# A feed-forward output product cut by token tiles instead of by output columns

## The chip, the cores and the metric

The kernel runs on one core of one Trainium2 chip, in fp32 throughout: matrix products are made of fp32r parts, as described below. The metric is the device time of one execution in microseconds. The kernel before has a median of 1441.0 us over 3 runs.

## What is computed

One step of an encoder layer on 640 tokens (512 of a prompt, 128 of eight samples of 16) with a model width of 1024. Two feed-forward blocks stand around a token mixer; each is followed by a gated, normalised residual. The parts that the change touches are the second half of the feed-forward block and what comes right behind it:

```python
def swiglu(h, w_in, w_out):
    gate, up = jnp.split(h @ w_in, 2, axis=-1)
    return (jax.nn.silu(gate) * up) @ w_out          # D_FF = 2816 -> 1024

def residual(x, out, g, gate, weight):
    return x + weight * gate[:, None, :] * rms_norm(out, g)

def trunk_layer(...):
    x = residual(x, swiglu(modulate(x, ...), w_ffn1_in, w_ffn1_out), ..., 0.5)
    heads, new_state = mixer(modulate(x, ...))       # modulate begins with rms_norm(x)
    x = residual(x, heads @ w_out, ..., 1.0)
    x = residual(x, swiglu(modulate(x, ...), w_ffn2_in, w_ffn2_out), ..., 0.5)
    return x, new_state
```

The root mean square of a token's output row is taken over all 1024 columns. So nothing of the residual of a token can be finished before all columns of its output are.

## The kernel before

The program is written engine by engine; each engine runs its instructions in the order of the code and waits on counting semaphores. Tokens are 5 tiles of 128 (`NT`), tiles 0 to 3 of the prompt, tile 4 of the samples. The hidden width is 22 blocks of 128 (`FT`), kept transposed in `act_t` (`ACTT`), one block of 640 tokens after the other. Numbers f = 0 and f = 1 are the two feed-forward blocks.

The output product (`ffn_out`) runs over the 22 hidden blocks in 11 turns (`OUT_TURNS`) of two slots, s = 0 and s = 1. For a slot, SP loads a block of the weight into `w_raw` (`RAW`); ACT rounds it to fp32r (`w_hi`) and the tokens' block too (`act_hi`), in `out_hi`; DVE subtracts to get the low parts (`w_lo`, `act_lo`), in `out_lo`; and PE makes three matmuls for each pair of a token tile and 512 columns: high times high, high tokens with low weight, low tokens with high weight. `k_landed`, `k_hi`, `k_lo` and `k_mm` count the loads, the high parts, the low parts and the slots that PE is done with. Each slot has one place in every buffer, so ACT may write the next turn's high parts of slot s only when PE is done with that slot (`k_mm[s]`), and SP may reload its `w_raw` only when both low parts are made.

The 640 x 1024 output takes 10 banks of PSUM, of which there are 8, 512 fp32 columns each. The kernel before therefore makes the product in two halves of columns: 11 turns with all 5 token tiles and columns 0 to 511 (banks 0 to 4), then 11 turns with the same tiles and columns 512 to 1023. Per slot that is 15 matmuls of 128x512. In the first 6 turns of f = 0 other small products (adaLN parameters, `ada_mm`, `ada_tr`) stand between the slots; a few transposes for the gate rows (`gate_mms`) stand in turns 6 and 7.

Behind each half ACT squares the five banks with a sum over the columns (`y_squares`), and DVE multiplies them with the gate rows into `y` (`y_gated`). Behind the second half follow, in this order: `inverse_mean` on DVE and a square root on ACT; on DVE `resid` += `y` times the root, five tiles of 128x1024; and, for f = 0, the next norm: ACT squares each new `resid` tile, DVE and ACT invert and take the root, DVE scales three tiles into `x_norm` and ACT two; only then PE transposes `x_norm` for the mixer (`norm` on PE waits for all five tiles). For f = 1 the new `resid` tiles are stored instead (L641), and that ends the kernel.

The product in front of this one (`ffn_in`) ends with sums on DVE that empty banks 0 to 6, a silu on ACT and the last block of `act_t` on DVE; `out_hi(0, 0)` and `out_lo(0, 0)` are placed among these last steps.

All three matmul forms are recorded under one line, the helper `mm` at L1079, and all subtractions under L1723.

## Time and profile before

| | us |
|---|---|
| median of 3 runs (1438.35 to 1442.01) | 1441.0 |
| the profiled execution | 1432.52 |
| its span, first to last instruction | 1430.7 |
| PE busy in the span | 1317.1 (92%) |
| DVE busy | 828.3 (58%) |
| ACT busy | 573.1 (40%) |
| mean granted TensorE clock | 0.952 |

The span is what the trace shows; the execution's own time is 1.8 us longer. The profiled execution is 8.5 us below the median of the runs, so a sum made from the trace is a difference to be applied to both, and not a time by itself. Busy shares are averages over the whole kernel. The stages of interest here are the two output products, at 359 to 522 us and 1265 to 1419 us of the span, and the stretches right behind them.

### The profile page before, as it was taken

Reading aid. Unit: us, or ns where it says so; the run is one execution under the profiler, and the core shown is the slowest. Engines: PE = TensorE matmul, PEld = TensorE weight load, DVE = VectorE, ACT = ScalarE, POOL = GpSimd, SP = SyncE. Lnnn points to the kernel's source line nnn. Section 1 sums busy time; section 2 is a strip of 40 time slices with the busy share of each in tenths; the row PEclk is TensorE's granted clock in tenths of the full one; section 3 lists DMA queues with packets and bytes.
Section 4 is the critical chain, followed back from the end, with each engine's and each line's share of the span. In section 5 each row is a group of like instructions: output and inputs, shape, how many; then the busy total and the mean of one; then the engine's idle time right before and its main releaser. Section 6 shows DMA issues by size and latency. Waiting matters only on the chain.

```text
span 1430.7 us, 23707 instructions
## 1 busy us (share of the span) xinstructions
PE 1317.1 (92%) x8072; PEld 1147.1 (80%) x8072; DVE 828.3 (58%) x1445; ACT 573.1 (40%) x1131; POOL 319.4 (22%) x276
## 2 busy tenths in 40 slices
PE   4999999999999969999997688969999999999996
PEld 2889999999778858888875355858899999988885
DVE  2666767776435455513335875338777777754545
ACT  4533434433334355322112465336444444433433
POOL 0443343433100000000100604004444444510000
PEclk9999999999999989999975698989999999999998
DMA  9545454544433322221220523112223322212232
GB/s 316 166 148 154 153 159 143 153 147 132 163 109 96 132 63 91 88 88 59 104 60 0 156 75 123 31 73 60 74 73 88 88 87 73 74 59 74 95 132 111
DMA packets 167003, 152.71 MB, mean 107 GB/s; under 512 B 10361, under 2 KB 139777, under 8 KB 166954
## 3 DMA queue, kind: packets, MB, share of 16 engines
q1 hardware_dynamic: 165610, 148.24, 33.0%
q0 software_dynamic: 1344, 3.81, 1.0%
q8 instruction: 31, 0.51, 0.2%
q14 instruction: 18, 0.15, 0.0%
HBM read 142.72 MB, written 9.05 MB: 106 GB/s over the span
## 4 chain that ended last, share of the span: by engine, by line
PE 79%; DVE 10%; issue 4%; ACT 4%; DMA 2%; DVEq 0%; POOL 0%; SPq 0%; ACTq 0%; POOLq 0%
PE ps L1079 76%; DVE resid L1942 1%; DVE w_sums_lo L1723 1%; DVE h_sums_lo L1723 1%; DVE max_den L2217 1%; DMA resid<-in_x_sample 1%; DMA w_raw<-in_w_ffn_in 1%; DVE act_t L1834 1%; DVE silu_gate L1827 1%; DVE w_lo L1723 1%; DVE probs L2226 1%; ACT x_norm L661 1%; PE ps L1121 0%; DVE y L1905 0%; ACT modulated_pairs L712 0%
## 5 line engine op out<-in xcount | busy, mean ns | idle before, releaser
L1079 PE MATMUL ps<-h_sums_hi,w_sums_hi 128*128 128x320 f32 x1216 | 378.0, 315 | 15.3 <-ACT silu_gate L731 5.0
L1079 PE MATMUL ps<-h_sums_hi,w_sums_lo 128*128 128x320 f32 x1216 | 370.7, 309 | 0.0
L1079 PE MATMUL ps<-h_sums_lo,w_sums_hi 128*128 128x320 f32 x1216 | 370.5, 309 | 0.0
L1079 PEld LDWEIGHTS ps<-h_sums_hi,w_sums_hi 128*128 128x128 f32 x1216 | 227.2, 188 | 31.9 <-issue 20.7
L1723 DVE TENSOR_TENSOR w_lo<-w_raw,w_hi 128x512 fp32r<-128x512 f32 (+3 forms) x106 | 99.0, 934 | 230.7 <-ACT w_hi L805 156.1
L1079 PEld LDWEIGHTS ps<-h_sums_lo,w_sums_hi 128*128 128x128 f32 x1216 | 227.2, 188 | 0.0
L1079 PEld LDWEIGHTS ps<-h_sums_hi,w_sums_lo 128*128 128x128 f32 x1216 | 227.1, 188 | 0.0
L1079 PE MATMUL ps<-w_hi,act_hi 128*128 128x512 f32 x440 | 174.0, 395 | 3.6 <-issue 3.6
L1079 PE MATMUL ps<-w_hi,act_lo 128*128 128x512 f32 x440 | 172.1, 391 | 0.0
L1079 PE MATMUL ps<-w_lo,act_hi 128*128 128x512 f32 x440 | 172.1, 391 | 0.0
L1723 DVE TENSOR_TENSOR w_sums_lo<-w_raw,w_sums_hi 128x512 fp32r<-128x512 f32 x136 | 129.1, 955 | 54.8 <-ACT w_sums_hi L749 45.0
L1723 DVE TENSOR_TENSOR w_sums_lo<-w_s,w_sums_hi 128x512 fp32r<-128x512 f32 x160 | 143.2, 895 | 4.3 <-ACT w_sums_hi L749 3.7
L753 ACT ACTIVATE silu_gate<-silu_gate 128x320 f32<-128x320 f32 x80 | 37.8, 472 | 254.4 <-DVE silu_gate L1827 254.4
L1079 PE MATMUL ps<-w_hi,h_t_hi 128*128 128x512 f32 (+2 forms) x360 | 135.2, 376 | 2.7 <-ACT h_t_hi L687 1.4
L1079 PE MATMUL ps<-w_lo,h_t_hi 128*128 128x512 f32 (+2 forms) x360 | 132.4, 368 | 0.0
L1079 PE MATMUL ps<-w_hi,h_t_lo 128*128 128x512 f32 (+2 forms) x360 | 132.4, 368 | 0.0
L805 ACT ACTIVATE w_hi<-w_raw 128x512 fp32r<-128x512 f32 x88 | 55.6, 632 | 175.9 <-PE ps L1079 154.2
L2326 POOL TENSOR_TENSOR w_s<-w_raw 128x512 f32<-128x512 f32 x40 | 54.7, 1369 | 296.5 <-DMA w_raw<-in_w_ffn_in 275.4
L749 ACT ACTIVATE w_sums_hi<-w_s 128x512 fp32r<-128x512 f32 x160 | 96.5, 625 | 34.9 <-POOL w_s L2329 24.2
L1079 PEld LDWEIGHTS ps<-w_hi,act_hi 128*128 128x128 f32 x440 | 83.0, 189 | 23.6 <-issue 6.9
L1079 PEld LDWEIGHTS ps<-w_hi,act_lo 128*128 128x128 f32 x440 | 82.9, 188 | 17.8
L1079 PEld LDWEIGHTS ps<-w_lo,act_hi 128*128 128x128 f32 x440 | 83.0, 189 | 16.9
(325 smaller groups left out, 1902.0 us busy)
## 6 DMA issues: line engine op xcount, KB each, us to landing
w_raw<-in_w_ffn_in SPq DMA_DIRECT2D x88, 512.0 KB, 3.8
w_raw<-in_w_ada SPq DMA_DIRECT2D x28, 1024.0 KB, 5.1
w_raw<-in_w_ffn_out SPq DMA_DIRECT2D x88, 256.0 KB, 2.6
w_raw<-in_w_in SPq DMA_DIRECT2D x10, 1024.0 KB, 5.1
w_raw_start<-in_w_ada SPq DMA_DIRECT2D x8, 1024.0 KB, 8.1
w_raw<-in_w_out SPq DMA_DIRECT2D x4, 1024.0 KB, 5.1
k_cache<-in_cache_k SPq DMA_DIRECT2D x8, 512.0 KB, 4.5
v_cache<-in_cache_v SPq DMA_DIRECT2D x8, 512.0 KB, 3.7
```

Source lines behind the costliest of these rows:

```text
L661: act.activation(XN[:, t, :], X[:, t, :], ACT.Square, accum_out=SS[:, 0, t:t + 1]).then_inc(x_sq, 1)
L749: act.activation(WHF[:, j, :, :], W_SOURCE[j], ACT.Copy).then_inc(w_hi, 1)
L753: act.activation(SIL[:, j * HALF:(j + 1) * HALF], SIL[:, j * HALF:(j + 1) * HALF], ACT.Silu).then_inc(f_silu, 1)
L805: act.activation(WH[:, 0, s * 1024:s * 1024 + 512], RAW[:, 0, s * 1024:s * 1024 + 512], ACT.Copy).then_inc(k_hi[s], 1)
L1079: return pe.matmul(out, lhsT, rhs, start=start, stop=stop)
L1723: return dve.tensor_tensor(dst, raw, hi.bitcast(F32), ALU.subtract)
L1827: dve.tensor_tensor(out, PS[:, bank, 0:HALF], other[:, :], ALU.add).then_inc(f_up, 1)
L1834: q = dve.tensor_tensor(ACTT[:, bass.ds(m, 1), cols].rearrange("p m n -> p (m n)"), SIL[:, cols], UP[:, j, :], ALU.mult)
L1942: dve.scalar_tensor_tensor(X[:, t, :], Y[:, t, :], RS[:, 1, t:t + 1], X[:, t, :], ALU.mult, ALU.add).then_inc(x_new, 1)
L2217: link(dve.reduce_max(MX[:, m:m + 2], ps, AXX))
L2226: link(dve.tensor_scalar(p0, p0, MX[:, m + 6:m + 7], None, ALU.mult))
L2326: pool.tensor_tensor(WS1[:, :, :], A21, A22, ALU.add).then_inc(w_sums, 1)
```

## The change

The output is cut the other way. The first 11 turns make token tiles 0, 1 and 2 with all 1024 columns, in six banks (0, 1, 2, 3, 4, 6); the next 11 turns make tiles 3 and 4 with all columns, in four banks (5, 7, 0, 1). A slot has 18 matmuls in the first group and 12 in the second, 660 per feed-forward block as before. Each slot now loads and splits 1024 columns of the weight instead of 512, and 384 or 256 tokens instead of 640.

Within a slot PE makes the high-high pass over all tiles and column halves first, then the two others, and waits for each kind of part only ahead of its pass. The last slot of a group goes tile by tile.

In the second group every buffer has two places q, used in turn: the weights of odd turns lie in the second half of `RAW`, `WH` and `WL`, the tokens' parts in columns 0 to 255 of `ASTH` and `ASTL`. ACT may thus write a turn's high parts when PE is done with the turn before the last one (`k_mm` of n - 1 instead of n), and SP may load when the turn before the last has its low weight parts. The Fori loops of the second group are written out on PE, ACT and DVE.

The squares, gating, residual addition and, for f = 0, the squares and scaling of the next norm of tiles 0 to 2 are placed between the slots of the second group, on ACT and DVE. Behind the last slot only those of tiles 3 and 4 are left. The reload of `resid` (L554) moves into the first group. The first `out_hi` of a block waits for six of the last turn's seven products instead of one, since its weight part is now twice as wide and lies on one more of their operands. The first slot's second matmul waits for the last block of `act_t` (`f_act`), which was waited for by its third tile before.

```diff
-        def out_view(T, s):
-            return T[:, 0, s * 1024:s * 1024 + 512]
+        def out_view(T, s, q=0):
+            return T[:, q, s * 1024:(s + 1) * 1024]
+
+
+        LATE = (OUT_TURNS + 1) // 2
+
+        def out_act(T, s, group, q=0):
+            return T[:, s, 0:2 * P] if q else T[:, s, OUT_COLS[group]]
+
+        def act_tile(T, s, t, q=0):
+            at0 = (t - OUT_TILES[1][0] if q else t) * P
+            return T[:, s, at0:at0 + P]
+
+        def out_landed(s, t, f, group):
+            if group == 0:
+                return k_landed[s], 16 * (t + ((OUT_TURNS + LATE) * f + 1))
+            if t % 2:
+                return l_landed[s], 16 * ((OUT_TURNS - LATE) * f + t // 2 + 1)
+            return k_landed[s], 16 * ((OUT_TURNS + LATE) * f + OUT_TURNS + t // 2 + 1)
+
+
+        OUT_TILES = ((0, 1, 2), (3, 4))
+        OUT_COLS = (slice(0, 3 * P), slice(3 * P, TOK))
+
+        def out_bank(t, half):
+            return (0, 1, 2, 3, 4, 6, 5, 7, 0, 1)[2 * t + half]
+
+        def y_count(r, t, half):
+            return 2 * NT * r + (NT * half + t if r == 1 else 2 * t + half) + 1
...
+                        for t in range(OUT_TURNS):
+                            n = (2 * f + 1) * OUT_TURNS + t
+                            if t == 1 and f == 0:
+                                sp.wait_ge(a_mm, FT + ADA_OUT)
+                            for s in range(2):
+                                if t != 1:
+                                    used = n - 1 if t == 0 else n - 2
+                                    sp.wait_ge(k_hi[s], 2 * used + 1)
+                                    sp.wait_ge(k_lo[s], 2 * used + 1)
+                                sp.dma_start(out_view(RAW, s, t % 2), ffn_out[f][(2 * t + s) * P:(2 * t + s + 1) * P, :]).then_inc(out_landed(s, t, f, 1)[0], 16)
...
+                        for t in range(ADA_OUT, OUT_TURNS):
                             turn(t)
-                            if t >= 2:
-                                back = x_spill[:, t - 2, :] if f else x_p[:, t - 2, :] if t - 2 < NTP else x_s
-                                sp.dma_start(X[:, t - 2, :], back).then_inc(x_landed, 16)
-                        with sp.Fori(NT + 2, OUT_TURNS) as t:
...
-                out_hi(0, 0, 2 * f * OUT_TURNS)
+                act.wait_ge(f_p, 7 * (f + 1) * REG + 4 * (f + 1) - 1)
+                out_hi(0, 0, f, 0)
...
-            def out_hi(s, t, n):
-                act.wait_ge(k_landed[s], 16 * (n + 1))
-                act.wait_ge(k_mm[s], n)
-                act.activation(WH[:, 0, s * 1024:s * 1024 + 512], RAW[:, 0, s * 1024:s * 1024 + 512], ACT.Copy).then_inc(k_hi[s], 1)
-                act.activation(ASTH[:, s, :], ACTT[:, bass.ds(2 * t + s, 1), :].rearrange("p a n -> p (a n)"), ACT.Copy).then_inc(k_hi[s], 1)
+            def out_hi(s, t, f, group):
+                n = t + (2 * f + group) * OUT_TURNS
+                q = t % 2 if group else 0
+                act.wait_ge(*out_landed(s, t, f, group))
+                act.wait_ge(k_mm[s], n - 1 if group and t else n)
+                act.activation(out_view(WH, s, q), out_view(RAW, s, q), ACT.Copy).then_inc(k_hi[s], 1)
+                cols = OUT_COLS[group]
+                act.activation(out_act(ASTH, s, group, q), ACTT[:, bass.ds(2 * t + s, 1), cols].rearrange("p a n -> p (a n)"), ACT.Copy).then_inc(k_hi[s], 1)
...
+                n1 = (2 * f + 1) * OUT_TURNS
+                out_hi(0, 0, f, 1)
+                tile_squares(f, 0)
+                tile_squares(f, 1)
+                out_hi(1, 0, f, 1)
+                tile_squares(f, 2)
+                for t in range(1, OUT_TURNS):
                     for s in range(2):
-                        out_hi(s, t, n0 + t)
+                        out_hi(s, t, f, 1)
+                    if t == 2:
+                        y_root(2 * f, 0, slice(0, 3))
+                    if f == 0 and 5 <= t < 8:
+                        if t == 5:
+                            for s in range(2):
+                                act.wait_ge(k_lo[s], 2 * (n1 + 4))
+                        row_squares(t - 5)
+                    if f == 0 and t == 8:
+                        row_root(0, slice(0, 3))
                 roots_table()
-                y_squares(2 * f, 1, out_bank(f, 1))
-
-            def residual(r):
-                act.wait_ge(y_ms, r + 1)
-                act.activation(RS[:, 1, :], SS[:, 1, :], ACT.Sqrt).then_inc(y_rstd, 1)
-
-
+                tile_squares(f, 3)
+                tile_squares(f, 4)
+                y_root(2 * f, 1, slice(3, 5))
+                if f == 0:
+                    for t in (3, 4):
+                        row_squares(t)
+                    row_root(1, slice(3, 5))
+                    act.wait_ge(x_rstd, rows_roots(1, 1))
+                    act.activation(XN[:, 4, :], X[:, 4, :], ACT.Copy, scale=RS[:, 0, 4:5]).then_inc(x_norm, 1)
...
+            def out_tile(s, q, passes, start, stop, t, half):
+
+                th, tl = act_tile(ASTH, s, t, q), act_tile(ASTL, s, t, q)
+                cols = slice(half * 512, (half + 1) * 512)
+                for i in passes:
+                    a, w = ((th, WH), (th, WL), (tl, WH))[i]
+                    done = mm(PS[:, out_bank(t, half), :], a, out_view(w, s, q)[:, cols], start and i == 0, stop and i == 2)
+                return done
+
+            def out_parts(s, n, i):
+
+                if i == 0:
+                    pe.wait_ge(k_hi[s], 2 * (n + 1))
+                else:
+                    pe.wait_ge(k_lo[s], 2 * n + i)
+
+            def out_mm(s, n, group, start=False, free=None, q=0):
+                for i in range(3):
+                    out_parts(s, n, i)
+                    for t in OUT_TILES[group]:
+                        for half in range(2):
+                            if free and i == 0:
+                                free(t, half)
+                            done = out_tile(s, q, (i,), start, False, t, half)
+                return done
+
+            def out_last(n, group):
+                for i in range(3):
+                    out_parts(1, n, i)
+                for t in OUT_TILES[group]:
+                    for half in range(2):
+                        done = out_tile(1, 0, range(3), False, True, t, half)
+                        if not (t == OUT_TILES[group][-1] and half):
+                            done.then_inc(out_done, 1)
+                done.then_inc(k_mm[1], 1)
...
+                    def free(t, half):
+
+                        if group and t == 3 and half == 0:
+                            pe.wait_ge(gate_rows, 8 * f + 4)
+                        elif group and t == 4:
+                            pe.wait_ge(y_copied, 4 * NT * f + half + 1)
+                        elif not group and t == 0:
+                            if half:
+                                pe.wait_ge(f_up, 7 * (f + 1) * REG)
+                                pe.wait_ge(f_act, (f + 1) * FT)
+                            else:
+                                pe.wait_ge(f_cp, (f + 1) * REG)
...
+            def out_lo(s, t, n, group):
+                q = t % 2 if group else 0
                 dve.wait_ge(k_hi[s], 2 * n + 1)
+                split_lo(out_view(WL, s, q), out_view(RAW, s, q), out_view(WH, s, q)).then_inc(k_lo[s], 1)
                 dve.wait_ge(k_hi[s], 2 * n + 2)
+                cols = OUT_COLS[group]
+                split_lo(out_act(ASTL, s, group, q), ACTT[:, bass.ds(2 * t + s, 1), cols].rearrange("p a n -> p (a n)"),
+                         out_act(ASTH, s, group, q)).then_inc(k_lo[s], 1)
...
+                n1 = n0 + OUT_TURNS
+                r = 2 * f
+                out_lo(0, 0, n1, 1)
+                tile_gated(r, 0)
+                tile_gated(r, 1)
+                out_lo(1, 0, n1, 1)
+                tile_gated(r, 2)
+                for t in range(1, OUT_TURNS):
                     for s in range(2):
-                        out_lo(s, t, n0 + t)
-                y_gated(2 * f, 1)
+                        out_lo(s, t, n1 + t, 1)
+                    if t == 1:
+                        inverse_mean(1, slice(0, 3), y_sq, y_count(r, 2, 1), y_ms)
+                    if 3 <= t < 6:
+                        if t == 3:
+                            dve.wait_ge(y_rstd, roots(r, 0))
+                        add_tile(r, t - 3)
+                    if f == 0 and t == 7:
+                        inverse_mean(0, slice(0, 3), x_sq, NT + 3, x_ms)
+                    if f == 0 and t >= 8:
+                        norm_row(t - 8, 0)
+                tile_gated(r, 3)
+                tile_gated(r, 4)
+                inverse_mean(1, slice(3, 5), y_sq, y_count(r, 4, 1), y_ms)
+                dve.wait_ge(y_rstd, roots(r, 1))
+                for t in (3, 4):
+                    add_tile(r, t)
+                if f == 0:
+                    inverse_mean(0, slice(3, 5), x_sq, 2 * NT, x_ms)
+                    norm_row(3, 1)```

What stands now at the end of the product on DVE, f = 0, first before and then after. `y` is the gated output, `resid` the residual, 128x1024 one token tile; the `w_lo`, `act_lo` rows are the slots of the last turns.

```order
180 L1723 TENSOR_TENSOR act_lo<-act_t,act_hi 128x640
181 L1930 REGISTER_ALU
182 L1930 COMPARE_AND_BRANCH
183 L1905 TENSOR_TENSOR y<-ps,gate_rows 128x512 x5
184 L1729 TENSOR_TENSOR sum_squares<-sum_squares 128x5
185 L1730 TENSOR_SCALAR sum_squares<-sum_squares 128x5
186 L1731 RECIPROCAL sum_squares<-sum_squares 128x5
187 L1942 SCALAR_TENSOR_TENSOR resid<-y,rstd,resid 128x1024 x5
188 L1730 TENSOR_SCALAR sum_squares<-sum_squares 128x5
189 L1731 RECIPROCAL sum_squares<-sum_squares 128x5
190 L1737 TENSOR_SCALAR x_norm<-resid,rstd 128x1024 x3
191 L1758 SCALAR_TENSOR_TENSOR scale_t<-mod_t,g_norm_t 128x72
```

After, at the same place:

```order
221 L1826 TENSOR_TENSOR w_lo<-w_raw,w_hi 128x1024
222 L1826 TENSOR_TENSOR act_lo<-act_t,act_hi 128x256
223 L2033 TENSOR_SCALAR x_norm<-resid,rstd 128x1024
224 L2023 TENSOR_TENSOR y<-ps,gate_rows 128x512 x4
225 L1832 TENSOR_TENSOR sum_squares<-sum_squares 128x2
226 L1833 TENSOR_SCALAR sum_squares<-sum_squares 128x2
227 L1834 RECIPROCAL sum_squares<-sum_squares 128x2
228 L2029 SCALAR_TENSOR_TENSOR resid<-y,rstd,resid 128x1024 x2
229 L1833 TENSOR_SCALAR sum_squares<-sum_squares 128x2
230 L1834 RECIPROCAL sum_squares<-sum_squares 128x2
231 L2033 TENSOR_SCALAR x_norm<-resid,rstd 128x1024
232 L1861 SCALAR_TENSOR_TENSOR scale_t<-mod_t,g_norm_t 128x72
```

Behind the last slot stand two additions instead of five and one scaled tile instead of three; those of tiles 0 to 2 stand between slots further up.

The place between the two parts of the product, again DVE and f = 0, before:

```order
167 L1723 TENSOR_TENSOR w_lo<-w_raw,w_hi 128x512
168 L1723 TENSOR_TENSOR act_lo<-act_t,act_hi 128x640
169 L1905 TENSOR_TENSOR y<-ps,gate_rows 128x512 x5
170 L1723 TENSOR_TENSOR w_lo<-w_raw,w_hi 128x512
171 L1723 TENSOR_TENSOR act_lo<-act_t,act_hi 128x640
```

And after:

```order
167 L1826 TENSOR_TENSOR w_lo<-w_raw,w_hi 128x1024
168 L1826 TENSOR_TENSOR act_lo<-act_t,act_hi 128x256
169 L2023 TENSOR_TENSOR y<-ps,gate_rows 128x512 x4
170 L1826 TENSOR_TENSOR w_lo<-w_raw,w_hi 128x1024
171 L1826 TENSOR_TENSOR act_lo<-act_t,act_hi 128x256
172 L2023 TENSOR_TENSOR y<-ps,gate_rows 128x512 x2
```

The gating of the first group is now six pieces, four between the first two slots of the next group and two behind the second.

## Rows read from the trace of the kernel before

**Rows 1.** The page: shares of the chain that ended last, by engine.

```profile
PE 79%; DVE 10%; issue 4%; ACT 4%; DMA 2%; DVEq 0%; POOL 0%; SPq 0%; ACTq 0%; POOLq 0%
```

**Rows 2.** Windows: stretch, length, busy us of PE, PEld, DVE, ACT, POOL, clock, DMA share, GB/s.

```profile
426.00:521.70 95.70, 95.66 (x423) 78.70 (x421) 45.77 (x62) 41.43 (x76) 0.00 (x0) 1.00 0.34 109
521.70:534.20 12.50, 0.04 (x1) 0.07 (x2) 10.48 (x17) 9.03 (x17) 0.00 (x0) 0.64 0.07 19
1263.60:1265.50 1.90, 0.00 (x0) 0.01 (x1) 1.90 (x4) 1.38 (x3) 0.00 (x0) 1.00 0.00 0
1419.00:1430.70 11.70, 0.00 (x0) 0.00 (x0) 7.93 (x11) 0.92 (x4) 0.00 (x0) 0.67 0.56 224
```

**Rows 3.** The chain in order of time, second half of the first output product.

```profile
426.27 92.68 PE ps L1079 x408
```

**Rows 4.** Timeline behind the first output product: start, us, engine, what, [idle before].

```profile
521.69 0.60 ACT L821 ACTIVATE y<-ps 128x512 f32<-128x512 f32 x1
...
529.98 1.06 ACT L661 ACTIVATE x_norm<-resid 128x1024 f32<-128x1024 f32 x1
...
531.83 2.19 ACT L666 ACTIVATE x_norm<-resid,rstd 128x1024 f32<-128x1024 f32 x2
...
519.70 3.41 DVE L1905 TENSOR_TENSOR y<-ps,gate_rows 128x512 f32<-128x512 f32 x5 [2.50 <-ACT y L821]
...
523.88 6.07 DVE L1942 SCALAR_TENSOR_TENSOR resid<-y,rstd,resid 128x1024 f32<-128x1024 f32 x5 [0.27 <-ACT rstd L862]
531.16 0.17 DVE L1730 TENSOR_SCALAR sum_squares<-sum_squares 128x5 f32<-128x5 f32 x1 [1.22 <-ACT x_norm L661]
...
531.83 2.08 DVE L1737 TENSOR_SCALAR x_norm<-resid,rstd 128x1024 f32<-128x1024 f32 x3 [0.28 <-ACT rstd L663]
...
534.16 3.58 PE L1121 MATMUL ps<-const,x_norm 128*128 128x128 f32 x15 [12.51 <-ACT x_norm L666]
```

**Rows 5.** Windows of 1 us around the fall and the rise of the clock.

```profile
525.00:526.00 1.00, 0.00 (x0) 0.00 (x0) 1.00 (x2) 0.81 (x1) 0.00 (x0) 0.61 0.00 0
...
538.00:539.00 1.00, 0.94 (x5) 0.90 (x5) 0.62 (x1) 1.00 (x3) 0.00 (x0) 0.56 0.09 16
```

**Rows 6.** End of the kernel: DVE and SP timeline, then stores with median us to landing.

```profile
1421.21 6.07 DVE L1942 SCALAR_TENSOR_TENSOR resid<-y,rstd,resid 128x1024 f32<-128x1024 f32 x5 [0.27 <-ACT rstd L862]
...
1427.30 0.33 SPq L641 DMA_DIRECT2D out_y_sample<-resid  x1
...
out_y_prompt<-resid SPq DMA_DIRECT2D x4, 512.0 KB, 2.8
```

**Rows 7.** Timeline of DVE and PE where the first output product begins.

```profile
357.62 0.68 DVE L1723 TENSOR_TENSOR w_lo<-w_raw,w_hi 128x512 fp32r<-128x512 f32 x1
358.21 0.82 DVE L1723 TENSOR_TENSOR act_lo<-act_t,act_hi 128x640 fp32r<-128x640 f32 x1
358.95 0.48 DVE L1834 TENSOR_TENSOR act_t<-silu_gate,up 128x320 f32<-128x320 f32 x1
...
359.14 0.47 PE L1079 MATMUL ps<-w_hi,act_hi 128*128 128x512 f32 x1 [1.62 <-issue]
```

**Rows 8.** Timeline: ACT and DVE parts of 1056 columns, in the mixer.

```profile
536.26 1.07 ACT L883 ACTIVATE w_hi<-w_raw 128x1056 fp32r<-128x1056 f32 x1
...
537.37 1.26 DVE L1723 TENSOR_TENSOR w_lo<-w_raw,w_hi 128x1056 fp32r<-128x1056 f32 x1 [0.18 <-ACT w_hi L883]
```

**Rows 9.** The page: weight loads of 512 KB and 1024 KB, us to landing.

```profile
w_raw<-in_w_ffn_in SPq DMA_DIRECT2D x88, 512.0 KB, 3.8
w_raw<-in_w_ada SPq DMA_DIRECT2D x28, 1024.0 KB, 5.1
```

**Rows 10.** PE timeline, pairs of matmuls that share a weight and alternate banks.

```profile
72.43 0.46 PE L1079 MATMUL ps<-h_sums_hi,w_sums_hi 128*128 128x320 f32 x2
72.72 0.46 PE L1079 MATMUL ps<-h_sums_lo,w_sums_hi 128*128 128x320 f32 x2
```

**Rows 11.** The chain: one piece of the first product, runs of 12 matmuls in one bank.

```profile
1150.52 10.83 PE ps L1079 x72
```

184 lines of the change are left out of this document (90 added, 94 removed).

## The prediction

> **What bounds the kernel now.** I read the chain of work that ended last first: PE makes 79% of it [rows 1]. So time can come from two things only, fewer or cheaper matmuls, or shorter stretches in which PE has nothing to do. The windows say where those are. In the second half of the first output product PE is busy 95.66 us of 95.70 [rows 2]: no wait ends there, nor can one be taken away. 408 matmuls take 92.68 us, 0.227 us each [rows 3]; DVE is busy less than half of that stretch and ACT 43%. Right behind it PE does nothing for 12.5 us, and behind the last product of the kernel nothing more is there for PE: 11.7 us pass until the end [rows 2]. These two stretches are the ones that the change works on.
>
> The timeline shows what the 12.5 us consist of [rows 4]. PE ends at 521.65. ACT squares the last bank from 521.69; DVE gates it until 523.11 (519.70 + 3.41, 0.68 us a bank). Inverse and root take 0.77 us. From 523.88 DVE adds five tiles, 6.07 us or 1.21 us a tile. ACT squares each new tile as it comes; the last starts at 529.98, just behind the last addition (529.95). DVE can invert at 531.16, and from 531.83 DVE scales three tiles while ACT scales two, in 2.19 us. PE's first transpose comes at 534.16. The end of the kernel is the same up to the additions, which start at 1421.21; the last store is issued at 1427.30, when they are through, and the span ends 3.4 us later [rows 6].
>
> **What the change removes.** Tiles 0 to 2 leave both stretches.
> In the first, three of five additions go: 3 x 1.21 = 3.64 us. ACT scales one tile instead of two: 2.19 / 2 = 1.10 us. Everything else in that chain stays, since it hangs on the last bank and the last tile: the square, the gating, 0.77 us, two additions, one square of 1.18 us until DVE may go on, 0.67 us for inverse and root, one scaling, 0.14 us. With PE's end as zero: 1.46 (gated) + 0.77 + 2.43 = 4.66, + 1.21 = 5.87, + 0.67 = 6.54, + 1.10 + 0.14 = 7.8 us instead of 12.5. **4.7 us** saved.
> In the second, three additions go: 3.64 us, and the last store is issued that much earlier. Before, five stores came 1.21 us apart; now the last two are alone, and the median landing is 2.8 us beside about 3.1 of the last one [rows 6]. I take 0.1 for it: **3.7 us**.
>
> **What the change adds to the path.** Only the start of each product. Before, DVE made 512 weight columns (starts at 357.62, the next instruction at 358.21, so 0.59 us) and 640 tokens (0.74 us), and then the last half block of `act_t`, from 358.95 until 359.43; PE had started at 359.14 and did not need that block before its seventh matmul [rows 7]. Now the weight part has 1024 columns. The nearest row is the one of 1056 columns, 1.26 us on DVE [rows 8]; less the overlap of about 0.08 that the narrower ones show and scaled, 1.14 us. The tokens' part has 384 columns, 0.6 x 0.74 = 0.45 us. So `act_t` is finished at 357.62 + 1.14 + 0.45 + 0.48 = 359.69. PE can do one matmul before it and 17 behind it, so its stream is as if it had begun at 359.69 - 0.23 = 359.5 instead of 359.14: about 0.4 us lost, in each product. The second start has the same shape, with PE idle for 1.9 us [rows 2]. Together **0.8 us**.
>
> **What is costed at nothing, and its cover.** The matmuls: 660 per block before and after, same shape. Their order changes: now two neighbours share the stationary part and write different banks, and no bank gets two in a row except in the last slot. The first norm has such pairs: two matmuls of 320 columns every 0.29 us [rows 10], against 10.83 / 72 = 0.15 us each for twelve in one bank [rows 11]. So 0, between -0.005 and 0 us per matmul; that would be up to 6 us less if it were real for 1320 matmuls, but the 0.15 holds the tail of the last one.
> The feed: per slot ACT has now 1.07 us for the weight part [rows 8] and some 0.4 us for the tokens, DVE 1.2 and 0.3 to 0.45 us, so 1.5 and 1.6 us, against 18 x 0.227 = 4.1 us of PE in the first group and 12 x 0.227 = 2.7 us in the second. Cover is left: 60% and 40% of the time. Into the 40% (10 turns of 5.45 us) go what left the end: on DVE three additions, three scalings, six inverses' instructions, under 7 us; on ACT three squares and two roots, under 5 us. Without this cover they would cost as much as is saved. If one slot needed both engines in a row on a single place, 1.5 + 1.6 = 3.1 us would not fit into 2.7 us; this is what the two places are for. With them a high part may be written two turns after the last use of its place, so the 3.1 us have over 5 us.
> The loads: 512 KB a slot instead of 256 KB. A load of 512 KB lands in 3.8 us, one of 1024 KB in 5.1 us [rows 9]. In the first group, single place, slot s of turn t is loaded when the low parts of turn t - 1 are made, 3.1 us behind `k_mm` of turn t - 2; it is wanted as high part one turn and one slot later, 8.2 + 4.1 us behind that `k_mm`, less 1.5 us for ACT. So a load has 7.7 us before PE waits. In the turns with the adaLN products a turn is longer, by more than 1 us, and one more 1024 KB load is in flight; 5.1 us plus a share of 3.8 stays below. In the second group a load has over 15 us. So 0, and the bound above is in the rivals.
> The change from one group to the other: six banks must be squared (0.68 us each, 4.1 us) and gated (4.1 us), and beside that ACT and DVE must feed four slots before they are ahead. Counted from the begin of the first group's last slot, ACT does slot 0 (1.4 us), four squares, then slot 1 from 4.2 (its `k_mm` comes there), two squares, and the third slot's high part by 8.5 us; PE wants it at 4.1 + 2 x 2.7 = 9.5 us. DVE has the low weight part by about 9.7, PE wants it at 10.4 us. The first two gated banks are free at 3.5 and 4.2 us, wanted at 4.5 and 4.8 us. So no wait, but with 0.5 to 1 us to spare; before, that place had five banks in 3.4 us, and slots of 3.4 us.
>
> **The sum.** -4.7 - 3.7 + 0.8 = **-7.6 us**. Against its own profile: 1432.52 becomes 1424.9, and the span 1430.7 becomes 1423.1. The median of the runs shown is 8.5 us above that profile; the same difference gives 1441.0 - 7.6 = **1433.4 us**, 0.53% less. A change of under 0.3% (4.3 us) could hardly be told from none.
>
> **The clock.** PE's clock fell from 2.4 to 1.2 GHz about 3.6 us after PE had stopped (mean 0.61 between 525 and 526) and came back at about 538.9, 4.7 us after the transposes began [rows 5]. A stretch of 7.8 us is still longer than 3.6 us, so the transposes will begin slowly again, and I take nothing from it. 15 transposes take 3.58 us there; at the higher level up to half of that, and not all of it on the path, so at most about 1.5 us more could be won.
>
> **Rivals.**
> *The change of groups gives it back.* If ACT or DVE is late by more than the 0.5 to 1 us that I count, PE waits once per block, and ACT and DVE catch up within a turn or two. A queue late by 2.5 us costs about 1.5 to 2 us a block, 3 to 4 us in all: result -3.6 to -4.6 us, 1437 us, at the edge of what can be told. For it: four queues meet there, each in its order, and the margins are made of sums of ten durations. Against it: PE waited nowhere in the halves' change before [rows 2]. 0.2.
> *The loads become the bound; the kernel is slower.* If the load of a slot in the second group cannot overlap with the next, a slot takes 3.8 us instead of 2.7: 1.1 us x 44 slots = 47 us more, 1480 us. It decides once a load takes longer than a slot and they come one by one. Against it: the five last stores, 512 KB each, went out 1.21 us apart and each landed after 2.8 us [rows 6], so loads do overlap; and 1024 KB in 5.1 us is less than a turn of 5.45 us. Weaker forms, in the turns with adaLN loads, cost 1 us a turn, 6 us, and just reach no gain. 0.1 for all of them, half of that slower.
> The Trainium skill speaks for this rival (DMA: Bandwidth & Descriptors, "Anatomy of one DMA"): a transfer costs about 2.0 us plus its bytes over 436 GB/s, so an estimate of 3.2 us for 512 KB, longer than a slot; one by one that would be 0.5 us x 44 = 22 us more. The trace has 3.8 us for such a load, which is longer still, and by its stores it shows that the fixed part overlaps.
> *More than counted.* The clock stays up or comes back sooner (1.5 us), or matmuls are cheaper in alternate banks (up to 6 us): 1427 to 1432 us. 0.12.
> *The change doesn't do what it says.* Additions placed between slots could wait for a late reload of `resid`, or hold up the slots behind them: no gain at the ends and 4 us of waits inside, 1441 to 1445 us. DVE waits in the third turn for the root of ACT, and `w_lo` of later slots stands behind it. 0.06.
> The forecast itself has 0.52, and its own range is 1431 to 1436 us.
>
> **Range and chances.** From 1428.5 us (part of the cheaper matmuls) to 1441 us (the groups' change, or a weaker form of the load rival). What lies outside is the loads as a bound, small parts of the others and a shift of the runs' level by itself. Faster by over 0.3%: 0.52 + 0.12 + 0.09 of the first rival = 0.73. Within 0.3%: 0.10 of it, 0.05 of the loads, 0.02 of the last = 0.17. Slower: 0.01 of the first, 0.05 of the loads, 0.04 of the last = 0.10.
>
> **What the profile will show.** Right: PE busy all through both products but for starts of about 2 us; under 8 us idle before the first transpose of the mixer; about 8 us from the last matmul to the end; DVE busier inside the second group, three additions there. Wrong: PE idle with `w_hi`, `w_lo` or `y` as releaser at the sixth bank or the third slot of the second group; idle with `w_raw` behind it, periodic by slot; or more than 0.23 us per matmul. The prediction fails most easily if a small wait repeats each turn: 0.1 us in each of 44 slots of the second groups would take half of what is won.

## The result and the profile after

The changed kernel has a median of 1427.81 us over 20 runs (1421.08 to 1438.36), the kernel before one of 1435.82 us over 20 runs beside it (1428.60 to 1442.01). The ratio is 0.9949, with a 95% interval of 0.9930 to 0.9968: the change saves about 7.3 us by the ratio, 8.0 by the medians. The profiled execution took 1424.57 us, with a span of 1422.8 us where it was 1430.7.

So the forecast difference of -7.6 us was right, and the forecast time of 1433.4 us was not. The range began at 1428.5 us, and the measured median lies 0.7 us below it.

Windows of the changed kernel: first the second group of the first output product and the stretch behind it, then the second product and the end. The columns are those of [rows 2].

```profile
426.50:518.80 92.30, 92.30 (x416) 76.63 (x415) 55.46 (x75) 50.02 (x85) 0.00 (x0) 1.00 0.57 190
521.50:528.60 7.10, 0.00 (x0) 0.02 (x1) 4.85 (x11) 3.87 (x8) 0.00 (x0) 0.77 0.00 0
...
1263.50:1415.60 152.10, 151.46 (x675) 125.26 (x675) 79.60 (x102) 68.55 (x111) 4.19 (x9) 1.00 0.51 173
1415.60:1422.80 7.20, 0.00 (x0) 0.00 (x0) 3.69 (x7) 0.29 (x2) 0.00 (x0) 0.78 0.36 146
```

PE is again busy without a pause in the second group. DVE and ACT, at 60% and 54% of it, do more beside it than before, and the transfer share has risen from 0.34 to 0.57, but nobody makes PE wait. The timeline behind the first product, which answers to [rows 4] (start, us, engine, what, idle before):

```profile
519.50 2.73 DVE L2023 TENSOR_TENSOR y<-ps,gate_rows 128x512 f32<-128x512 f32 x4 [6.18 <-ACT y L879]
522.97 2.48 DVE L2029 SCALAR_TENSOR_TENSOR resid<-y,rstd,resid 128x1024 f32<-128x1024 f32 x2 [0.27 <-ACT rstd L884]
525.49 1.06 ACT L888 ACTIVATE x_norm<-resid 128x1024 f32<-128x1024 f32 x1
526.67 0.17 DVE L1833 TENSOR_SCALAR sum_squares<-sum_squares 128x2 f32<-128x2 f32 x1 [1.22 <-ACT x_norm L888]
527.32 1.15 ACT L942 ACTIVATE x_norm<-resid,rstd 128x1024 f32<-128x1024 f32 x1
528.61 3.58 PE L1196 MATMUL ps<-const,x_norm 128*128 128x128 f32 x15 [7.82 <-ACT x_norm L942]
```

Two additions stand where five stood, one square still follows the last of them, one scaling on ACT: the chain is what the prediction made of it, link for link, and the idle stretch is 7.82 us (forecast 7.8). The end, which answers to [rows 6], with the median us to landing of the last store:

```profile
1417.15 2.48 DVE L2029 SCALAR_TENSOR_TENSOR resid<-y,rstd,resid 128x1024 f32<-128x1024 f32 x2 [0.27 <-ACT rstd L884]
...
1419.66 0.33 SPq L686 DMA_DIRECT2D out_y_sample<-resid  x1
...
out_y_sample<-resid SPq DMA_DIRECT2D x1, 512.0 KB, 2.7
```

From the last matmul (ends at 1414.97) to the end of the span 7.83 us pass; it was 11.71. The start of the first product, which answers to [rows 7]:

```profile
356.43 1.22 DVE L1826 TENSOR_TENSOR w_lo<-w_raw,w_hi 128x1024 fp32r<-128x1024 f32 x1
357.56 0.55 DVE L1826 TENSOR_TENSOR act_lo<-act_t,act_hi 128x384 fp32r<-128x384 f32 x1
358.03 0.48 DVE L1937 TENSOR_TENSOR act_t<-silu_gate,up 128x320 f32<-128x320 f32 x1
...
356.19 0.48 PE L1154 MATMUL ps<-w_hi,act_hi 128*128 128x512 f32 x1
358.66 1.40 PE L1154 MATMUL ps<-w_hi,act_hi 128*128 128x512 f32 x5 [2.00 <-DVE act_t L1937]
```

PE makes one matmul and then waits 2.00 us for the last block of `act_t`, which stands behind two subtractions on DVE.

The whole span can be cut at six marks: the end of each `ffn_in`, the last matmul of each output product, the first transpose and the first product of the mixer. In us of the profiled executions, worked out from the timelines; the stretch ahead of the first mark holds the rest:

| kernel | product 1 | idle | transposes | mixer and `ffn_in` | product 2 | tail | span |
|---|---|---|---|---|---|---|---|
| before | 164.49 | 12.50 | 6.40 | 723.00 | 155.43 | 11.71 | 1430.7 |
| changed | 164.80 | 7.82 | 6.39 | 725.83 | 154.14 | 7.83 | 1422.8 |
| residual late | 164.80 | 12.50 | 6.39 | 723.87 | 154.16 | 11.73 | 1430.7 |
| one place | 170.85 | 7.83 | 6.39 | 722.21 | 162.00 | 8.22 | 1435.4 |
| late wait | 162.75 | 7.82 | 6.39 | 726.88 | 152.09 | 7.82 | 1420.0 |
| two `w_raw` only | 165.25 | 7.82 | 6.39 | 727.33 | 156.06 | 7.82 | 1426.4 |
| all parts first | 166.64 | 7.82 | 6.39 | 729.45 | 155.98 | 7.82 | 1431.8 |
| both of these | 169.55 | 7.82 | 6.39 | 725.10 | 160.59 | 7.84 | 1433.2 |

The columns of the idle stretch and of the tail are the same to 0.02 us in every kernel with the same chain, but for the tail of one place (8.22 us, with the same chain up to the last store). The mixer's column, in which no kernel differs in its work, moves by 7 us: how much of it is the clock is told below. So a verdict on a mechanism is read from the stretch that it works on.

The product columns hold a piece of clock, too. Seven of these kernels begin each product with a pause of PE of 1.6 to 2.4 us, all but the late wait. Behind 7 of these 14 pauses the granted clock is at 1.2 GHz for 3.4 us; it falls between 0.3 us before the pause ends and 1.4 us after. The row is that of the kernel before, behind the pause that ends at 1265.52 (columns as above):

```profile
1265.90:1269.30 3.40, 3.40 (x10) 2.62 (x9) 2.25 (x3) 0.00 (x0) 3.27 (x7) 0.50 0.26 82
```

At half the clock such a piece costs 1.7 us. It stands in product 1 of one place and of all parts first, and in product 2 of before, one place, two `w_raw` only, all parts first and both of these. The changed kernel and the residual late have none, and the late wait, whose longest pause there is 0.28 us, has none either. In the comparisons below these 1.7 us are taken off where they stand. That the pause brings the fall is likely from these counts; no experiment shows it.

### The profile page after: what moved, and what is told of

Same layout as the page of the kernel before. It is cut to its first block, busy times and chain, and to the rows that moved or that the text cites. A ratio compares the mean times of both kernels' runs of the same rounds, so it can differ in the third digit from the quotient of the medians.

```text
span 1422.8 us, 23263 instructions
## 1 busy us (share of the span) xinstructions
PE 1318.9 (93%) x8072; PEld 1148.1 (81%) x8072; DVE 831.8 (58%) x1454; ACT 583.8 (41%) x1133; POOL 319.4 (22%) x276
## 4 chain that ended last, share of the span: by engine, by line
PE 80%; DVE 9%; issue 4%; ACT 4%; DMA 2%; DVEq 0%; POOL 0%; SPq 0%; ACTq 0%; POOLq 0%
PE ps L1154 76%; DVE w_sums_lo L1826 1%; DVE h_sums_lo L1826 1%; DVE max_den L2356 1%; DMA resid<-in_x_sample 1%; DMA w_raw<-in_w_ffn_in 1%; DVE act_t L1937 1%; DVE w_lo L1826 1%; DVE silu_gate L1930 1%; PE ps L1196 1%; DVE probs L2365 1%; DVE resid L2029 1%; ACT x_norm L706 0%; ACT modulated_pairs L757 0%; DVE y L2023 0%
## 5 line engine op out<-in xcount | busy, mean ns | idle before, releaser
L1154 PE MATMUL ps<-h_sums_hi,w_sums_hi 128*128 128x320 f32 x1216 | 377.9, 315 | 14.5 <-DVE silu_gate L1930 4.6
L1154 PE MATMUL ps<-h_sums_hi,w_sums_lo 128*128 128x320 f32 x1216 | 370.8, 309 | 0.0
L1154 PE MATMUL ps<-h_sums_lo,w_sums_hi 128*128 128x320 f32 x1216 | 370.7, 309 | 0.0
L1826 DVE TENSOR_TENSOR w_lo<-w_raw,w_hi 128x1024 fp32r<-128x1024 f32 (+2 forms) x106 | 145.8, 1375 | 205.4 <-ACT w_hi L852 130.6
L1154 PEld LDWEIGHTS ps<-h_sums_hi,w_sums_hi 128*128 128x128 f32 x1216 | 226.9, 188 | 31.5 <-issue 21.5
L1154 PEld LDWEIGHTS ps<-h_sums_lo,w_sums_hi 128*128 128x128 f32 x1216 | 227.3, 188 | 0.0
L1154 PEld LDWEIGHTS ps<-h_sums_hi,w_sums_lo 128*128 128x128 f32 x1216 | 227.2, 188 | 0.0
L852 ACT ACTIVATE w_hi<-w_raw 128x1024 fp32r<-128x1024 f32 x88 | 93.2, 1059 | 147.4 <-PE ps L1154 124.4
L1826 DVE TENSOR_TENSOR w_sums_lo<-w_raw,w_sums_hi 128x512 fp32r<-128x512 f32 x136 | 120.8, 894 | 54.9 <-ACT w_sums_hi L794 45.1
L1826 DVE TENSOR_TENSOR w_sums_lo<-w_s,w_sums_hi 128x512 fp32r<-128x512 f32 x160 | 143.2, 895 | 4.4 <-ACT w_sums_hi L794 4.0
L1154 PE MATMUL ps<-w_hi,h_t_hi 128*128 128x512 f32 (+2 forms) x360 | 135.7, 377 | 2.8 <-DVE h_t_lo L1826 1.7
L1154 PE MATMUL ps<-w_hi,h_t_lo 128*128 128x512 f32 (+2 forms) x360 | 132.9, 369 | 0.0
L1154 PE MATMUL ps<-w_lo,h_t_hi 128*128 128x512 f32 (+2 forms) x360 | 132.7, 369 | 0.0
L2464 POOL TENSOR_TENSOR w_s<-w_raw 128x512 f32<-128x512 f32 x40 | 60.3, 1507 | 296.5 <-DMA w_raw<-in_w_ffn_in 275.4
L1154 PE MATMUL ps<-w_hi,act_hi 128*128 128x512 f32 x440 | 119.3, 394 | 4.4 <-DVE act_t L1937 4.4
L1154 PE MATMUL ps<-w_lo,act_hi 128*128 128x512 f32 x440 | 117.0, 390 | 0.0
L1154 PE MATMUL ps<-w_hi,act_lo 128*128 128x512 f32 x440 | 116.6, 389 | 0.0
L1154 PEld LDWEIGHTS ps<-w_hi,act_hi 128*128 128x128 f32 x440 | 81.2, 188 | 23.7 <-issue 7.4
L794 ACT ACTIVATE w_sums_hi<-w_raw 128x512 fp32r<-128x512 f32 x120 | 74.7, 624 | 54.3 <-DMA w_raw<-in_w_ffn_in 51.7
L1154 PEld LDWEIGHTS ps<-w_lo,act_hi 128*128 128x128 f32 x440 | 82.6, 188 | 17.5
## 6 DMA issues: line engine op xcount, KB each, us to landing
w_raw<-in_w_ffn_in SPq DMA_DIRECT2D x88, 512.0 KB, 3.8
w_raw<-in_w_ffn_out SPq DMA_DIRECT2D x88, 512.0 KB, 3.6
w_raw<-in_w_ada SPq DMA_DIRECT2D x28, 1024.0 KB, 5.0
w_raw<-in_w_in SPq DMA_DIRECT2D x10, 1024.0 KB, 5.1
w_raw_start<-in_w_ada SPq DMA_DIRECT2D x8, 1024.0 KB, 8.5
w_raw<-in_w_out SPq DMA_DIRECT2D x4, 1024.0 KB, 5.1
k_cache<-in_cache_k SPq DMA_DIRECT2D x8, 512.0 KB, 5.0
v_cache<-in_cache_v SPq DMA_DIRECT2D x8, 512.0 KB, 3.7
```

The costliest lines, as they stand in the source:

```text
L794: act.activation(WHF[:, j, :, :], W_SOURCE[j], ACT.Copy).then_inc(w_hi, 1)
L852: act.activation(out_view(WH, s, q), out_view(RAW, s, q), ACT.Copy).then_inc(k_hi[s], 1)
L1154: return pe.matmul(out, lhsT, rhs, start=start, stop=stop)
L1826: return dve.tensor_tensor(dst, raw, hi.bitcast(F32), ALU.subtract)
L2464: pool.tensor_tensor(WS1[:, :, :], A21, A22, ALU.add).then_inc(w_sums, 1)
```

## The experiments

Theory A is the prediction: the gain is the two shortened chains, less a late start of each product; the second place of each buffer is needed to get it. Theory B is the rival that an experiment names in its place. The first four kernels ran together on one chip with 32 runs of the kernel before (median 1433.90 us), the last three on another with 23 runs (1435.88 us).

### The residual of tiles 0 to 2 behind the last slot again

```diff
-                    if 3 <= t < 6:
-                        if t == 3:
-                            dve.wait_ge(y_rstd, roots(r, 0))
-                        add_tile(r, t - 3)
...
-                for t in (3, 4):
+                for t in range(NT):
                     add_tile(r, t)
```

The inverses, roots, squares and scalings of these tiles move in the same way; the cut by token tiles and the two places stay.

> The changed kernel with the roots, additions, squares and scalings of tiles 0 to 2 moved back behind the last slot; the cut by token tiles, the two places and the gating between the groups stay. Theory A (the gain is only the shorter chains behind the two products): both stretches grow back to 12.5 us before the first transpose and about 11.7 us at the end; +4.7 and +3.8 us against the changed kernel, so within 2 us of the kernel before, ratio 1.000. Theory B (part of the gain is from the cut itself, the order of matmuls or the larger loads): stays faster than before by 2 us or more, ratio 0.998 or less, with PE's time inside the products shorter than 162.5 and 153.5 us.

Measured: 1433.59 us (12 runs), ratio 0.9998 (0.9973 to 1.0023). The profile has the old stretches back to the hundredth, an idle time of 12.50 us and a tail of 11.73:

```profile
534.55 3.58 PE L1188 MATMUL ps<-const,x_norm 128*128 128x128 f32 x15 [12.50 <-ACT x_norm L934]
```

So the cut by tiles by itself brings nothing that could be seen (the ratio leaves 3.6 us either way, the stretches hardly 0.1); what it allows, the placing of the residual between the slots, is the whole gain. The products have the same lengths as in the changed kernel (164.80, 154.16), so the work that was put between the slots costs PE nothing there.

### One place for every buffer in the second group

```diff
-                q = t % 2 if group else 0
+                q = 0
...
-                act.wait_ge(k_mm[s], n - 1 if group and t else n)
+                act.wait_ge(k_mm[s], n)
...
-                                if t != 1:
-                                    used = n - 1 if t == 0 else n - 2
+                                used = n - 1
```

> The changed kernel with one place for every buffer in the second group too. Theory A (the latency of a load needs the second place): landing, high part, low part and next load follow each other on one place, 1.0 + 1.2 + 3.8 us, about 6 us per turn where PE needs 5.45 us, so PE waits about 0.5 us in each of 10 turns per block, 10 us in all, more if the two slots' loads slow each other (up to 20 us): slower than before by 2 to 12 us, ratio 1.001 to 1.009. Theory B (the second place is of no use): as the changed kernel, ratio 0.995.

Measured: 1436.93 us (10 runs), ratio 1.0015 (0.9988 to 1.0042): the gain is gone. The products are 6.1 and 7.9 us longer than in the changed kernel. Of each, 1.7 us is the piece at 1.2 GHz at its start, so the single places cost 4.3 and 6.2 us, 10.5 together; the ratios differ by 9.5 us. ACT and PE at one of the waits, from their timelines:

```profile
503.34 1.06 ACT L847 ACTIVATE w_hi<-w_raw 128x1024 fp32r<-128x1024 f32 x1 [2.60 <-DMA w_raw<-in_w_ffn_out]
504.30 0.40 ACT L849 ACTIVATE act_hi<-act_t 128x256 fp32r<-128x256 f32 x1
...
504.75 1.20 PE L1149 MATMUL ps<-w_hi,act_hi 128*128 128x512 f32 x4 [1.89 <-ACT act_hi L849]
```

ACT waits 2.60 us for a load, and PE 1.89 us for ACT. In all PE waits 4.4 us in three places for `act_hi` and 2.8 us in two for `act_lo`. These are few waits, not one in each of 44 slots; the rest of the 10.5 us is small delays at other slots' begins, of up to 0.12 us. With one `w_raw` the next load can begin only when the low part is made. Here SP issued it at 500.72, when `w_lo` of that place had been made (until 500.65), and ACT stood idle from 500.74 until the load had landed. In most turns its latency fits into what is left of the turn; that a square or an addition on ACT or DVE is what makes it late in the others is a reading of the code, not tested.

### The wait for the last block of `act_t` later

```diff
                     out_parts(s, n, i)
+                    if free and i == 2 and group == 0:
+                        pe.wait_ge(f_act, (n // (2 * OUT_TURNS) + 1) * FT)
...
                                 pe.wait_ge(f_up, 7 * (f + 1) * REG)
-                                pe.wait_ge(f_act, (f + 1) * FT)
```

> The changed kernel, where PE waits for the last block of act_t only ahead of the first slot's third pass and not ahead of its second matmul. Theory A (this wait is what the start of each product costs): PE starts about 0.3 us behind the sums instead of 2.0 and 2.4 us, so 1.7 to 2.1 us less at each of the two starts, 3.6 us in all: ratio to the kernel before 0.992. Theory B (a low part or the high part of the second slot comes last there as well): the wait moves to w_lo or w_hi, and less than 1 us in all is won, ratio 0.995.

Measured: 1418.49 us (9 runs), ratio 0.9893 (0.9861 to 0.9925), the best of all. Windows of the first product (columns as above):

```profile
357.00:519.00 162.00, 162.00 (x795) 129.78 (x795) 84.15 (x116) 74.88 (x125) 4.28 (x9) 1.00 0.57 193
```

There is no pause in it any more; both products are 2.05 us shorter, 4.1 us together. The ratio says more, some 8 us against the changed kernel's ratio. The stretches bear out the 4.1 us. Part of the rest may be the pieces at 1.2 GHz, which stood behind half of the pauses of the other kernels: half of 2 x 1.7 us is 1.7 us on average, an estimate from 14 starts. The remainder, some 2 us, stays open; the intervals of the two ratios (0.9861 to 0.9925 here, 0.9930 to 0.9968) are 5 to 9 us wide.

### Two places of `w_raw`, one of the parts

```diff
-                act.wait_ge(k_mm[s], n - 1 if group and t else n)
-                act.activation(out_view(WH, s, q), out_view(RAW, s, q), ACT.Copy).then_inc(k_hi[s], 1)
+                act.wait_ge(k_mm[s], n)
+                act.activation(out_view(WH, s), out_view(RAW, s, q), ACT.Copy).then_inc(k_hi[s], 1)
```

The same for `w_lo`, `act_hi` and `act_lo`; the loads are those of the changed kernel.

> The changed kernel, where in the second group only w_raw has two places and the high and low parts have one. Theory A (as in the prediction: 1.5 us of ACT and 1.6 us of DVE in a row do not fit into the 2.7 us of the other slot): about 0.4 us of waiting in each of 40 slots, 16 us slower than the changed kernel, ratio 1.006. Theory B (since each pass waits for its own part only, the low parts may come 0.9 and 1.8 us into the slot and the chain fits): waits only in the turns with additions and squares in between, under 3 us in all, ratio 0.995 to 0.997.

Measured: 1428.07 us (10 runs), ratio 0.9961 (0.9940 to 0.9982). By time it is the changed kernel. In all of the trace PE waits for a part twice, 0.4 us in all, each time ahead of the last slot of a block, which goes tile by tile and so wants all its parts first. The products are 0.5 and 1.9 us longer, 1.7 of the latter by the clock. One of the waits, and the lines of the view of `act_lo` that say who waited for it:

```profile
517.98 0.47 PE L1154 MATMUL ps<-w_hi,act_hi 128*128 128x512 f32 x1 [0.18 <-DVE act_lo L1826]
```

```profile
who waited for it (us, times):
...
  PE ps L1154: 0.4, 2
```

The prediction's sentence that 3.1 us of ACT and DVE on a single place would not fit into a slot of 2.7 us is wrong. Of the second places only that of `w_raw` does work here.

### All parts awaited before the first matmul, three passes to a bank

```diff
-                for i in range(3):
+                for i in (0, 2):
                     out_parts(s, n, i)
-                    for t in OUT_TILES[group]:
-                        for half in range(2):
-                            if free and i == 0:
-                                free(t, half)
-                            done = out_tile(s, q, (i,), start, False, t, half)
+                for t in OUT_TILES[group]:
+                    for half in range(2):
+                        if free:
+                            free(t, half)
+                        done = out_tile(s, q, range(3), start, False, t, half)
```

> The changed kernel, but PE goes tile by tile inside a slot and waits for all four parts ahead of its first matmul, as the kernel before did. Theory B of the run with two raw places only (the passes cover the low parts) says that with two places of everything the order of the passes covers nothing: no wait in either product but up to 0.3 us at each start, ratio 0.995 as the changed kernel, product lengths 164.8 to 165.2 and 154.1 to 154.5 us. If instead banks in turn make matmuls cheaper, the products get longer by up to 3 us each.

Measured: 1429.71 us (10 runs), ratio 0.9962 (0.9940 to 0.9985): with all second places in use, as the changed kernel. The products are 1.8 us longer each in the profile, and both have the piece at 1.2 GHz at their start, 1.7 us each, so 0.1 us each is left. PE waits 0.2 us for a part in each second group, at its second slot, so "no wait in either product" was not quite right. The price of a matmul is read better from starts than from lengths. In the changed kernel, first at alternating banks, then in the last slot in runs of three to a bank (PE's timeline):

```profile
484.36 1.07 PE L1154 MATMUL ps<-w_hi,act_lo 128*128 128x512 f32 x4
485.26 1.07 PE L1154 MATMUL ps<-w_hi,act_hi 128*128 128x512 f32 x4
486.17 1.07 PE L1154 MATMUL ps<-w_lo,act_hi 128*128 128x512 f32 x4
...
519.94 0.39 PE L1154 MATMUL ps<-w_hi,act_hi 128*128 128x512 f32 x1
520.17 0.39 PE L1154 MATMUL ps<-w_lo,act_hi 128*128 128x512 f32 x1
```

Four matmuls in 0.905 us are 0.226 each, and from 519.94 to 520.17 it is 0.23: the order of the banks makes no matmul cheaper.

The same order with two places of `w_raw` only:

> Two places for w_raw only, and PE tile by tile with all parts waited for ahead of a slot. Theory B: now the low parts must be ready at the slot's begin, 2.6 to 2.8 us behind k_mm of the same slot, where the other slot gives 2.7 us; 0 to 0.2 us of wait in each of 40 slots, and 0.5 to 1 us more in the turns with additions: 4 to 12 us slower than the run with two raw places and passes (1426.4 us span), ratio 0.999 to 1.004. If the parts never mattered, ratio 0.996.

Measured: 1434.63 us (10 runs), ratio 0.9994 (0.9975 to 1.0013). The gain is gone, the products are 4.8 and 6.5 us longer than in the changed kernel, 4.8 each without the clock's 1.7 us in the second. The view of `act_lo`, and PE's timeline from the last matmul of one slot to the second of the next:

```profile
who waited for it (us, times):
...
  PE ps L1154: 2.6, 15
```

```profile
480.71 0.39 PE L1154 MATMUL ps<-w_hi,act_lo 128*128 128x512 f32 x1
481.25 0.47 PE L1154 MATMUL ps<-w_hi,act_hi 128*128 128x512 f32 x1
481.55 0.40 PE L1154 MATMUL ps<-w_lo,act_hi 128*128 128x512 f32 x1
```

This is the sum of 3.1 against 2.7 us, where it holds: when a slot needs all its parts at its begin. The view puts down only 2.6 us of waits, since the matmuls' ends in it are modelled. The starts tell more: from 480.71 to 481.25 are 0.54 us, where 0.23 is the rule, and from there to 481.55 are 0.30, so 0.4 us is lost at this slot's begin. It is so at the second slot (s = 1) of each of the 11 turns and not at the first, 4.3 us in each second group. That is most of the 4.8 us that each product has lost, at half as many slots and twice the price that the expectation gave. Why only the second slot waits was not looked into. So two things cover for each other: the second places of the parts, or the order of the passes. Either alone is enough; without both the kernel is as slow as before.

### The first transposes of the mixer in the idle stretch

On top of the late wait, PE makes the transposes of tiles 0 to 2 of the first block when their `x_norm` is there, and waits for tiles 3 and 4 behind them.

```diff
-                pe.wait_ge(x_norm, NT * (p + 1))
+                pe.wait_ge(x_norm, NT * p + 3 if p == 1 else NT * (p + 1))
...
+                            if p == 1 and k == 0 and t == 3:
+                                pe.wait_ge(y_copied, 2 * NT)
+                                pe.wait_ge(x_norm, 2 * NT)
```

> The run with the late wait for act_t, and in addition PE transposes tiles 0 to 2 of the first column block of x_norm as soon as these are there, ahead of tiles 3 and 4. From the rows of the changed kernel: a transpose takes 0.24 us behind the gap, so three of the five that stand between the last x_norm and ACT's first modulated block leave the path, 0.7 us less from the last matmul to the mixer's first product (14.2 us in the changed kernel). Rival: ACT and DVE, not the transposes, set the pace there and nothing is won. Against the kernel before 0.988 to 0.990; against the late wait alone not to be told apart by the median.

Measured: 1421.46 us (6 runs), ratio 0.9903 (0.9878 to 0.9927); it can't be told from the late wait alone (0.9893). PE's timeline:

```profile
520.54 0.52 PE L1199 MATMUL ps<-const,x_norm 128*128 128x128 f32 x3 [1.55 <-issue]
526.81 2.94 PE L1199 MATMUL ps<-const,x_norm 128*128 128x128 f32 x12 [5.75 <-ACT x_norm L942]
```

From the last matmul to the mixer's first product 13.58 us pass instead of 14.21, so the part does what it should, 0.63 us, and that is too little to see in a median. Three transposes didn't keep the clock up over the 5.75 us behind them: it is at 1.2 GHz when the twelve begin, and they take 0.245 us each, where the fifteen of the changed kernel take 0.239. The window of this run (columns as above):

```profile
522.50:526.80 4.30, 0.00 (x0) 0.02 (x1) 2.39 (x5) 3.65 (x6) 0.00 (x0) 0.51 0.00 0
```

## Why the difference was right and the time was not

**The first idle stretch**: 4.7 us forecast, 4.68 measured (12.50 to 7.82). **The tail**: 3.7 forecast, 3.88 measured; the 0.2 more is that the last of two stores at the end lands 0.3 us sooner than the last of five, where 0.1 was taken. **The starts**: 0.4 us each forecast. The idle time is 2.00 and 2.4 us; against a start without it the late wait shows 2.05 us each. Against the kernel before, from the end of `ffn_in` to the start of the second matmul, 2.67 and 2.68 us pass instead of 2.27 in both: 0.40 and 0.41 us, 0.8 for 0.8. What the forecast didn't name is that such a pause can bring 3.4 us at 1.2 GHz with it; before and after both have the pause, so nothing had to be taken for it in a difference. **The sum**: -7.6 forecast; -7.3 by the ratio, -8.0 by the medians. The four stretches that the change works on come to +0.3 - 4.7 + 0.4 - 3.9 = -7.9 us with the clock's 1.7 us taken off product 2 of the kernel before.

The spans differ by 7.9 us as well, and the forecast had 1424.9 us for an execution like the profiled one, which took 1424.57. That this fits to 0.3 us is luck: the spans also hold 1.7 us of clock in product 2 of the kernel before, 1.2 us less ahead of the first product, which nothing here explains, and 2.8 us more in the mixer's column, and these three nearly cancel.

**The change of groups**: no wait there, as forecast; that rival is out. **The loads**: 512 KB landed in 3.6 us, and with two places PE has no wait in either product that goes back to one. With one place they do cost time, but not as the rival had it: there no load was to overlap with the next, in every slot, for 47 us; here the landing of a load is late in a few turns, for 4.3 + 6.2 = 10.5 us in both products. The second place of `w_raw` shuts that out. The estimate of 3.2 us for such a load, made with the fit of the Trainium skill (DMA: Bandwidth & Descriptors, "Anatomy of one DMA"), is below the 3.6 and 3.8 us of the traces. The page gives that fit for transfers that GpSimd issues, and these are issued by SP, so it was applied outside its case; no term of the sum hung on it. That loads overlap, as the stores did, is shown by slots of 2.7 us fed by loads of 3.6. **Cheaper matmuls**: not there, 0.226 us each in alternating banks, 0.227 before.

**"This is what the two places are for"**: wrong, as told; the sum of ACT and DVE is the wrong thing to hold against a slot when PE asks for the high parts first and for the low parts one third and two thirds of a slot later. It holds only together with the order of the passes, as the run with both shows.

**What failed** is the last step, "The median of the runs shown is 8.5 us above that profile; the same difference gives 1441.0 - 7.6". It took the median of three runs for the kernel's level. Twenty runs of the same kernel have a median of 1435.82, 5.2 us lower. 1435.82 - 7.6 would have been 1428.2 us, 0.4 us from the measured median. The mechanism and the sum of the difference were right; the term that was mis-sized is the level that it was taken from. And the range had bounds for every mechanism, but for this step nothing: "a shift of the runs' level by itself" was named and left outside. The runs of the kernel before scatter from 1428.4 to 1442.0 us, which is nearly twice the whole gain, and those three (1438.35 to 1442.01) came from the upper part of that. The profiled execution of 1432.52 us, 8.5 us below them, was a sign that three runs did not fix the level.

What the scatter goes with is the clock. Over the 32 runs of before on one chip the mean granted clock goes from 0.943 to 0.956 and the time follows it, 0.95 us for each 0.001 (correlation -0.92); over the 23 on the other 1.09 us (-0.90). That is a correlation, worked out from the runs' records, and no experiment held the clock; but the code is the same in all of them. The traces show where it happens: the mixer's stretch, with the same work, lasts 722 to 729 us, and the longest pieces of it at 1.2 GHz lie 180 to 290 us behind its begin. These 105 us had a mean clock of 0.63 in the kernel with the shortest mixer's column (one place, 722.21) and of 0.58 in the one with the longest (all parts first, 729.45):

```profile
728.00:833.00 105.00, 82.79 (x349) 55.60 (x347) 69.76 (x178) 34.11 (x117) 24.88 (x28) 0.63 0.24 64
```

```profile
723.60:828.60 105.00, 83.20 (x339) 57.03 (x340) 66.13 (x167) 30.12 (x106) 25.54 (x30) 0.58 0.26 70
```

In the kernel before the second product had its piece as well and was busy 153.47 us where the changed kernel has 151.75. So 1.7 us of what the second product's column seems to win is the clock of one execution, and the late start is hidden behind it.

**The clock behind the idle stretch**: forecast was that the transposes begin slowly again. They do. Windows of the changed kernel (columns as above):

```profile
524.00:525.00 1.00, 0.00 (x0) 0.00 (x0) 1.00 (x2) 0.71 (x1) 0.00 (x0) 1.00 0.00 0
525.00:526.00 1.00, 0.00 (x0) 0.00 (x0) 0.45 (x1) 0.95 (x3) 0.00 (x0) 0.68 0.00 0
526.00:528.60 2.60, 0.00 (x0) 0.02 (x1) 1.23 (x4) 1.99 (x4) 0.00 (x0) 0.50 0.00 0
528.60:531.00 2.40, 2.39 (x11) 2.12 (x12) 0.58 (x2) 0.97 (x2) 0.00 (x0) 0.50 0.00 0
...
535.00:537.00 2.00, 2.00 (x11) 2.00 (x12) 1.97 (x4) 1.63 (x3) 0.00 (x0) 0.65 0.59 208
537.00:539.00 2.00, 2.00 (x12) 2.00 (x11) 1.93 (x6) 0.43 (x1) 0.00 (x0) 0.50 0.56 138
539.00:541.00 2.00, 2.00 (x18) 2.00 (x18) 1.16 (x3) 1.12 (x3) 0.00 (x0) 0.99 0.39 133
```

PE stops at 520.79, and the clock falls from 2.4 to 1.2 GHz some 4.6 us later (3.6 us in the kernel before, and 2.1 to 4.6 us over the kernels of the table). It comes back while the transposes run and then falls a second time, so that the mixer's first products run at 1.2 GHz until 539: 21 matmul records in 4 us, where 29 stood at the higher level in the kernel before. From the mixer's first product to its third set of transposes 5.11 us pass (535.00 to 540.11), where 4.02 passed in the kernel before (540.56 to 544.58): 1.1 us lost. Why it falls again in some executions stays open. In the first 4 us of the mixer the clock was 1.00 before, with one place, with the late wait and with both combined (two `w_raw`, all parts first); 0.58 in the changed kernel and 0.55 with the early transposes; 0.50 with the residual late, with two `w_raw` only and with all parts first only. Both lengths of the idle stretch, 12.5 and 7.8 us, stand on both sides.

## What to carry to other kernels

Look for work behind a product that needs only some of its rows, and cut the product so that these rows are ready early; the gain can be counted link by link from the chain, to 0.2 us here. When such a cut doubles a load per slot, find out which of the second places is for latency and which only for a sum of engine times, since an order of passes may cover the latter. Look at the clock of a stretch before a length is read as waiting: here 1.7 us of several product lengths was the clock. A forecast time needs a level, and a few runs of a kernel whose clock wanders do not give one: state the difference, and let the range include the scatter of the runs at its full width.
